# A row of table entries for the score banks of differential attention, and a bank of its own for five heads' sums of squares

## The chip, the cores and the metric

One Trainium2 chip, one core. The metric is the device time of one execution in microseconds (us), the median of several runs. TensorE is called PE here, VectorE DVE, ScalarE ACT, GpSimd POOL and SyncE SP, as in the profile. PSUM, the memory that PE writes and ACT and DVE read, has eight banks of 512 float32 per partition.

## The reference, cut to what matters

The kernel computes two transformer blocks of two layers each on 512 tokens of width 1024. The change touches one step of it, the differential attention of the second block: 8 heads, each with two score maps whose softmaxes are subtracted, and an RMS norm of each head's output over its 128 values.

```python
q_blk = q[:, i * BLOCK:n_k]
s = jnp.einsum('bqhcd,bkhcd->bhcqk', q_blk, k[:, :n_k]).astype(f32) * scale
s = jnp.where(kpos[None, :] <= qpos[:, None], s, -jnp.inf)
p = jax.nn.softmax(s, axis=-1)
a = p[:, :, 0] - lam * p[:, :, 1]
outs.append(jnp.einsum('bhqk,bkhe->bqhe', a.astype(v.dtype), v[:, :n_k]))
...
o = rms_norm_2(o, sub_gain) * (1.0 - lam_init)
```

The blocks i of 128 queries are causal: block b sees (b + 1) * 128 keys.

## The kernel before, in words

The whole kernel is one program in which every engine has its own instruction list, and semaphores hold them together. `X.wait_ge(e["name"], past(n))` lets engine X go on when n steps called "name" are done. An engine takes its instructions in their order, so a wait holds up all that stands behind it.

The differential attention is the functions `diff` of each engine: PE at line 1480, ACT at 2149, DVE at 2853, POOL at 859. Its unit is the **slot** s, one head h and one block b of queries: s = 4h + i, with b = i in head 0 and b = 3 - i in the others (`diff_slot`, line 728). So a head begins with its widest slot, of 512 keys, and ends with its narrowest, of 128. There are 32 slots. For one slot:

- PE `scores(s)` (lines 1510 to 1530) makes both maps c = 0, 1 with four matmuls each, of which one adds the mask. It waits until slot s - 3 has been read (`probs` past 2s - 4).
- DVE `neg_max(s)` (line 2889) takes the maxima of both maps from PSUM, and ACT `probs(s)` (line 2152) makes two exponentials of it, from PSUM to the tile tmp.
- DVE `combine(s)` (line 2897) forms the difference of the two maps. PE `turn_map(s)` (line 1532) transposes it in b + 1 blocks of 128 into bank 6, and ACT `take_map(s)` (line 2163) copies bank 6 to the tile Z.

Once a head: PE `values(h)` (line 1542) multiplies the four transposed maps with the values into bank 7. ACT `square(h)` (line 2171) squares bank 7. PE `mean_square(h)` (line 1551) sums these squares over the partitions with a matmul of ones (line 1556, two instructions) and adds the eps term in four small ones (line 1559, eight instructions), all into bank 6. ACT `scale(h)` (line 2177) makes a logarithm of bank 6 (line 2181) and an exponential (line 2184), which is the factor of the RMS norm. DVE `sub_norm(h)` and ACT `y_high(h)` use it.

Bank 6 therefore serves two things, the transposed maps and the sum of squares. Two waits keep them apart: `mean_square(h)` waits until the map before it has been taken (line 1554), and `turn_map` waits for the logarithm (line 1537).

The scores have banks 0 to 5, two banks a slot, in turn (`diff_pair`, line 736). From slot 20 on (line 733) a table gives them banks 0 to 4, where a slot of at most 256 keys has both maps in one bank. Bank 5 is then free for `fill`: from slot 24 on PE puts six matmuls of the output projection into every slot (lines 1487 to 1508, call at 1574), which write bank 5 (and bank 4 at the end).

The order of the work on PE is written out by hand at lines 1564 to 1578. In step s stand `turn_map(s - 3)`; then, in the last step of a head, `mean_square(h - 1)`; then `scores(s + 2)`; in the third step of a head `values(h - 1)`; and from step 24 on `fill(6)`. ACT's order is at lines 2196 to 2217: in step s `square(h - 1)` in the last step of a head, `scale(h - 2)` in the first, then `take_map(s - 3)`, then `probs(s)`.

Of the kernel before, what the change touches and what calls it, by code (L numbers as in the profile page):

```python
# [12 lines left out]
ACT = mybir.ActivationFunctionType  # L13
AX = mybir.AxisListType

P = 128
S = 512
# [3 lines left out]
NB = S // P  # L21
# [101 lines left out]
def program(nc, a, out):  # L123
# [9 lines left out]
    def past(n):  # L133

        return n + CR

    with ctx:
# [31 lines left out]
        ones = onesr[:, :].bitcast(F32)  # L169
        sq9 = sb("squares", [P, 5 * P])  # L170
        ident, ntri, nones, cos_rows, sin_rows = (sq9[:, k * P:(k + 1) * P] for k in range(5))
# [49 lines left out]
        PS = ctx.enter_context(nc.psum_tensor("banks", [P, 8 * S], F32))  # L221
        bank = [PS[:, j * S:(j + 1) * S] for j in range(8)]
        G = bank[0:2]

        def zt(k, n=1):
            return Z[:, k * S:(k + n) * S] if isinstance(k, int) else Z[:, bass.ds(k * S, n * S)]
# [419 lines left out]
        def tile_evac(st, b):  # L646

            return st.base // 2 + b // 2
# [76 lines left out]
        DIFF_SLOTS = 8 * NB  # L725
        BEHIND = 3
# [3 lines left out]
            h, i = divmod(s, NB)  # L730
            return h, i if h == 0 else NB - 1 - i

        PACKED = 5 * NB
        packed = dict(enumerate(((0, 1), (2, 3), (4,), (0,), (1, 2), (3, 4), (0,), (2,), (3, 4), (0, 1), (2,), (3,)), PACKED))

        def diff_pair(s):

            o = packed[s][0] if s >= PACKED else 2 * ((s + 1) % 3)
            step = S // 2 if s >= PACKED and len(packed[s]) == 1 else S
            return PS[:, o * S:o * S + 2 * step].rearrange("p (c n) -> p c n", n=step)  # L740

        def diff_scores(s, c):

# [2 lines left out]
        def fill_bank(l):  # L746

            return bank[4 if l in (5, 7) else 5]

        def fill_order(l):  # L750

            return {0: None, 6: 4, 7: 5}.get(l, l - 1 if l != 5 else None)
# [23 lines left out]
        def diff_eps(s, n=1):  # L776

            return sums8[:, 28 + s % 8:28 + s % 8 + n]
# [204 lines left out]
        def _(pe):  # L983
# [259 lines left out]
            for c in range(DC):  # L1243
# [3 lines left out]
                for b in range(NB):  # L1247
                    mm = pe.transpose(bank[5 + c % 2][:, b * P:(b + 1) * P], Z[:, 6 * S + b * D + c * P:6 * S + b * D + (c + 1) * P], ident)
# [231 lines left out]
            def diff(st):  # L1480
                e = df
                last = next(st for st in panels if st.ends == "diff")
                pe.wait_ge(h_take, past(last.tiles))

                filled = [0]

                def fill(n):

                    for m in range(filled[0], filled[0] + n):
                        l, i = divmod(m, 3 * FILL)  # L1490
                        k, part = divmod(i, 3)
                        par, u = l % 2, st.base + l
                        if i == 0:
                            if fill_order(l) is not None:
                                old = st.base + fill_order(l)
                                pe.wait_ge(evac[old % 2], past(old // 2 + 1))
                            if l == 5:
                                pe.wait_ge(e["probs"], past(2 * DIFF_SLOTS - 6))
                            if l == 0:
                                pe.wait_ge(e["output_high"], past(FILL))  # L1500
                                pe.wait_ge(e["output_low"], past(FILL))
                            pe.wait_ge(s_whi, past(u + 1))
                            pe.wait_ge(s_wlo, past(u + 1))
                        w, y = ((whi, yhi), (wlo, yhi), (whi, ylo))[part]
                        mm = pe.matmul(fill_bank(l), w[par][:, k * P:(k + 1) * P], ch(y, k), start=i == 0, stop=i == 3 * FILL - 1)
                        if i == 3 * FILL - 1:
                            mm.then_inc(gemm, 1)
                    filled[0] += n

                def scores(s):  # L1510

                    h, b = diff_slot(s)
                    n = (b + 1) * P
                    q_hi, q_lo, k_hi, k_lo = diff_parts(h)
                    pe.wait_ge(e["low_parts"], past(3 * h + 3))
                    if s in (NB, 2 * NB):
                        zero_rows_in(4)
                    if s in (1, 2):
                        for tile in (2 * s - 2, 2 * s - 1):
                            pe.wait_ge(evac[tile % 2], past(tile_evac(last, tile) + 1))  # L1520
                    pe.wait_ge(e["probs"], past(2 * s - 4))
                    qh, ql = q_hi[:, b * P:n], q_lo[:, b * P:n]
                    for c in range(2):
                        z = diff_scores(s, c)[:, 0:n]
                        kh, kl = k_hi[c][:, 0:n], k_lo[c][:, 0:n]
                        pe.matmul(z, qh, kh, start=True, stop=False)
                        pe.matmul(z, qh, kl, start=False, stop=False)
                        pe.matmul(z[:, b * P:n], identb[:, :], mask(M_C), start=False, stop=False, skip_group_check=True)
                        mm = pe.matmul(z, ql, kh, start=False, stop=True)
                    mm.then_inc(e["scores"], 1)  # L1530

                def turn_map(s):

                    h, b = diff_slot(s)
                    pe.wait_ge(e["combined"], past(s + 1))
                    pe.wait_ge(e["taken"], past(s))
                    pe.wait_ge(e["log_mean"], past((s + BEHIND - NB) // NB))
                    for kb in range(b + 1):
                        mm = pe.transpose(bank[6][:, kb * P:(kb + 1) * P], diff_probs(s, 0)[:, kb * P:(kb + 1) * P], ident)
                    mm.then_inc(e["turned"], 1)  # L1540

                def values(h):

                    pe.wait_ge(e["taken"], past(NB * h + NB))
                    pe.wait_ge(e["normed"], past(h))
                    for kb in range(NB):
                        mm = pe.matmul(bank[7][:, kb * P:S], zt(16 + h)[:, kb * P:(kb + 1) * P], zt(24 + kb)[:, kb * P:S],
                                       start=kb == 0, stop=kb == NB - 1, skip_group_check=True)
                    mm.then_inc(e["values_added"], 1)

                def mean_square(h):

                    pe.wait_ge(e["squares"], past(h + 1))
                    pe.wait_ge(e["taken"], past(min(NB * h + 2 * NB - BEHIND, DIFF_SLOTS)))
                    pe.wait_ge(e["eps_scaled"], past(h + 1))
                    pe.matmul(bank[6], ones, zt(28), start=True, stop=False, skip_group_check=True)
                    for s in range(NB * h, NB * h + NB):
                        _, b = diff_slot(s)
                        mm = pe.matmul(bank[6][:, b * P:(b + 1) * P], diff_eps(s).to_broadcast([P, P]), ident, start=False, stop=s == NB * h + NB - 1, skip_group_check=True)
                    mm.then_inc(e["mean_square"], 1)  # L1560

                scores(0)
                scores(1)
                for s in range(DIFF_SLOTS + BEHIND):
                    h, i = divmod(s, NB)
                    if s >= BEHIND:
                        turn_map(s - BEHIND)
                    if i == NB - 1 and h:
                        mean_square(h - 1)
                    if s + 2 < DIFF_SLOTS:  # L1570
                        scores(s + 2)
                    if i == (BEHIND - 1) % NB and h and s >= BEHIND:
                        values(h - 1)
                    if s >= 6 * NB:
                        fill(6)
                fill(12)
                mean_square(7)
                fill(18)

# [28 lines left out]
            for t in range(NB):  # L1608
                for hh in range(2):
                    n = 2 * t + hh  # L1610
                    if n >= 2:
                        pe.wait_ge(s_xc, DC + n - 1)
                    for c in range(4):
                        cc = 4 * hh + c
                        mm = pe.transpose(bank[n % 2][:, c * P:(c + 1) * P], xT[:, cc * S + t * P:cc * S + (t + 1) * P], ident)
# [5 lines left out]
        def _(act):  # L1621
# [527 lines left out]
            def diff(st):  # L2149
                e = df  # L2150
# [26 lines left out]
                def scale(h):  # L2177

                    act.wait_ge(e["mean_square"], past(h + 1))
                    act.wait_ge(e["rms_scale"], past(h))  # L2180
                    act.activation(zt(29), bank[6], ACT.Ln, scale=1.0 / P).then_inc(e["log_mean"], 1)
                    act.wait_ge(e["log_mean"], past(h + 1))
                    act.wait_ge(e["normed"], past(h))
                    act.activation(zt(30), zt(29), ACT.Exp, scale=-0.5).then_inc(e["rms_scale"], 1)
# [11 lines left out]
                for s in range(DIFF_SLOTS + BEHIND):  # L2196
                    h, i = divmod(s, NB)
# [814 lines left out]
```

## Time and profile before

| | us |
|---|---|
| three runs | 2924.63, 2926.41, 2929.20 |
| median | 2926.41 |
| span of the profiled execution | 2926.4 |
| differential attention in it | from 1418.9 to some 1543 |
| PE busy in the whole span | 2833.6 (97%) |

The profile gives the span of the profiled execution, from its first to its last instruction, and no other time of it. In a timeline a row has the start of an instruction, its duration, the engine and line, what it writes and reads, its shape and count; at the end, in brackets, stands the idle time of the engine before it and what released it. A PE row's duration runs over into the next one's start, since matmuls are pipelined: from start to start is what an instruction takes of PE's time.

### The profile page before, as it was taken

How to read it: one execution, taken by the hardware profiler on the slowest of the kernel's cores; microseconds unless marked ns; L12 is line 12 of the kernel's file. 1: busy time of each engine (PE TensorE's matmuls, PEld its weight loads, DVE VectorE, ACT ScalarE, POOL GpSimd, SP SyncE). 2: the span in 40 equal slices, each digit the busy share in tenths (PEclk: the TensorE clock that was granted, in tenths of full speed). 3: DMA queues.
4: the chain of work that ended last, by engine and by line, in shares of the span. 5: the costliest groups of instructions: out<-in, count | busy, mean ns of one | idle time of the engine just before them, and what ended most of it. 6: DMA issues, size and time to landing. Idle time of an engine off the chain costs nothing.

```text
span 2926.4 us, 39107 instructions
## 1 busy us (share of the span) xinstructions
PE 2833.6 (97%) x13399; PEld 2315.3 (79%) x13399; DVE 1744.8 (60%) x2111; ACT 1224.7 (42%) x2067; POOL 1079.0 (37%) x498
## 2 busy tenths in 40 slices
PE   6999999999899999999899999999999999999999
PEld 5767788887677888888667888888888888888887
DVE  7486777775566554668566333557566766644333
ACT  3574432224554322244454222356566665522221
POOL 1312344443213444444324444443412442244443
PEclk9999999999999999999999999999999999999999
DMA  6355263643112333332003333323301321133332
GB/s 218 88 167 193 79 203 98 208 127 105 37 30 79 93 99 95 94 95 87 29 26 97 94 94 95 99 88 91 92 23 53 95 87 30 51 94 94 101 94 93
DMA packets 366140, 278.96 MB, mean 95 GB/s; under 512 B 13618, under 2 KB 321203, under 8 KB 366003
## 3 DMA queue, kind: packets, MB, share of 16 engines
q1 hardware_dynamic: 364752, 276.83, 31.3%
q8 instruction: 82, 1.34, 0.2%
q14 instruction: 55, 0.45, 0.0%
q10 hardware_dynamic: 1251, 0.33, 0.0%
HBM read 275.03 MB, written 2.10 MB: 95 GB/s over the span
## 4 chain that ended last, share of the span: by engine, by line
PE 65%; issue 4%; DVE 2%; ACT 2%; POOL 1%; DMA 0%; POOLq 0%; DVEq 0%; ACTq 0%; SPq 0%
PE banks L1187 13%; PE banks L1182 12%; PE banks L1191 12%; PE banks L1050 6%; PE banks L1056 6%; PE banks L1053 6%; PE banks L1456 2%; PE banks L1023 1%; PE banks L1396 1%; PE banks L1184 1%; POOL w_lo L895 1%; PE banks L1385 0%; PE banks L1091 0%; PE banks L1431 0%; PE banks L1430 0%
## 5 line engine op out<-in xcount | busy, mean ns | idle before, releaser
L895 POOL TENSOR_TENSOR w_lo<-w_raw,w_hi 128x1024 fp32r<-128x1024 f32 (+2 forms) x431 | 1028.3, 2386 | 1693.2 <-ACT w_hi L1704 1692.2
L1704 ACT ACTIVATE w_hi<-w_raw 128x1024 fp32r<-128x1024 f32 (+2 forms) x432 | 447.3, 1035 | 1125.8 <-PE banks L1191 793.2
L1050 PE MATMUL banks<-w_hi,h_hi 128*128 128x512 f32 x960 | 386.4, 402 | 0.1
L1056 PE MATMUL banks<-w_lo,h_hi 128*128 128x512 f32 x960 | 376.7, 392 | 1.5 <-POOL w_lo L895 1.5
L1053 PE MATMUL banks<-w_hi,h_lo 128*128 128x512 f32 x960 | 375.2, 391 | 0.7 <-DVE h_lo L601 0.7
L1182 PE MATMUL banks<-h_hi,w_hi 128*128 128x512 f32 x1280 | 341.8, 395 | 7.1 <-ACT h_hi L1885 4.2
L1187 PE MATMUL banks<-h_lo,w_hi 128*128 128x512 f32 x1280 | 321.3, 391 | 2.4 <-DVE h_lo L601 2.3
L1182 PEld LDWEIGHTS banks<-h_hi,w_hi 128*128 128x128 f32 x1280 | 243.1, 190 | 65.0 <-issue 7.6
L1187 PEld LDWEIGHTS banks<-h_lo,w_hi 128*128 128x128 f32 x1280 | 240.5, 188 | 57.6 <-DVE h_lo L601 8.2
L1191 PE MATMUL banks<-h_hi,w_lo 128*128 128x512 f32 x1152 | 284.5, 389 | 0.0
L1191 PEld LDWEIGHTS banks<-h_hi,w_lo 128*128 128x128 f32 x1152 | 216.3, 188 | 44.9
L1182 PE MATMUL banks<-mid_hi,w_hi 128*128 128x512 f32 x864 | 220.3, 394 | 7.7 <-ACT mid_hi L1837 4.7
L1056 PEld LDWEIGHTS banks<-w_lo,h_hi 128*128 128x128 f32 x960 | 195.8, 204 | 36.9 <-POOL w_lo L895 3.2
L1053 PEld LDWEIGHTS banks<-w_hi,h_lo 128*128 128x128 f32 x960 | 196.6, 205 | 31.6 <-DVE h_lo L601 1.0
L1187 PE MATMUL banks<-mid_lo,w_hi 128*128 128x512 f32 x864 | 218.2, 391 | 2.3 <-DVE mid_lo L2394 2.1
L1050 PEld LDWEIGHTS banks<-w_hi,h_hi 128*128 128x128 f32 x960 | 196.1, 204 | 30.6 <-issue 0.5
L1191 PE MATMUL banks<-mid_hi,w_lo 128*128 128x512 f32 x864 | 214.4, 389 | 0.0
L2411 DVE TENSOR_TENSOR xT<-banks,xT 128x512 f32 (+1 forms) x80 | 55.3, 691 | 263.3 <-PE banks L1191 261.7
L1182 PEld LDWEIGHTS banks<-mid_hi,w_hi 128*128 128x128 f32 x864 | 160.7, 188 | 45.8 <-ACT mid_hi L1837 8.1
L1187 PEld LDWEIGHTS banks<-mid_lo,w_hi 128*128 128x128 f32 x864 | 162.2, 188 | 41.4 <-DVE mid_lo L2394 4.7
L1191 PEld LDWEIGHTS banks<-mid_hi,w_lo 128*128 128x128 f32 x864 | 162.2, 188 | 33.5
L2404 DVE TENSOR_TENSOR mid_lo<-tmp,mid_hi 128x512 f32 (+1 forms) x64 | 122.8, 1918 | 55.6 <-ACT mid_hi L1837 55.6
(373 smaller groups left out, 4272.8 us busy)
## 6 DMA issues: line engine op xcount, KB each, us to landing
Z<-in_ada_w SPq DMA_DIRECT2D x64, 512.0 KB, 5.2
w_raw<-in_m_w_up SPq DMA_DIRECT2D x64, 512.0 KB, 3.9
w_raw<-in_m_w_down SPq DMA_DIRECT2D x64, 512.0 KB, 3.6
w_raw<-in_kv_w SPq DMA_DIRECT2D x48, 512.0 KB, 3.8
w_raw<-in_ffn_w_gate SPq DMA_DIRECT2D x44, 512.0 KB, 3.7
w_raw<-in_ffn_w_up SPq DMA_DIRECT2D x44, 512.0 KB, 3.6
tmp<-in_ada_w SPq DMA_DIRECT2D x32, 512.0 KB, 4.4
w_raw<-in_ffn_w_down SPq DMA_DIRECT2D x32, 512.0 KB, 3.7
```

What stands on the lines that cost most here:

```text
L895: pool.tensor_tensor(wlo[j][:, 0:n], raw[j][:, 0:n], whi[j][:, 0:n], ALU.subtract).then_inc(s_wlo, 1)
L1023: mm = pe.transpose(turned(n)[:, j * P:(j + 1) * P], tmp[4 + n % 2][:, j * P:(j + 1) * P], ident)
L1050: pe.matmul(t, hh, wh, start=k == 0, stop=False)
L1053: pe.matmul(t, hl, wh, start=False, stop=False)
L1056: mm = pe.matmul(t, hh, wl, start=False, stop=k == DC - 1)
L1182: pe.matmul(g, whi[par][:, k * P:(k + 1) * P], hi[:, k * S:(k + 1) * S], start=(k == 0), stop=False)
L1187: mm = pe.matmul(g, whi[par][:, k * P:(k + 1) * P], lo[:, k * S:(k + 1) * S], start=False, stop=early and k == st.kc - 1)
L1191: mm = pe.matmul(g, wlo[par][:, k * P:(k + 1) * P], hi[:, k * S:(k + 1) * S], start=False, stop=(k == st.kc - 1))
L1456: mm = pe.matmul(o, dil_vals[:, at:at + P], dil_probs[q % 2][:, own:own + width], start=g == 0 and c == 0, stop=g == 2 and c == NB - 1, sk ...
L1704: act.activation(whi[par][:, 0:kc * P], raw[par][:, 0:kc * P], ACT.Copy).then_inc(s_whi, 1)
L2404: dve.tensor_tensor(ch(mlo, l), tmp[1], ch(mhi, l), ALU.subtract).then_inc(r_lo, 1)
L2411: dve.tensor_tensor(x, G[par], x, ALU.add).then_inc(evac[par], 1)
```

## The change

A table `PACKED` now gives the score banks of all 32 slots. Slots 0 and 1 have both maps in one bank each (2 and 3), slots 2 to 5 two banks each, slots 6 and 7 one bank each (5 and 4). Slots 8 to 31 use banks 0 to 4 alone, by the sequence that slots 20 to 31 had before. For heads 0 to 4 the sum of squares goes to bank 5 instead of bank 6. For these heads `mean_square` stands behind `scores(s + 2)` and not ahead of it, waits for the logarithm of the head before it and not for the map in bank 6, and `turn_map` waits for no logarithm. The first `fill`, which writes bank 5, waits for the logarithm of head 4. In slots 2 and 3 the waits for the banks of the stage before are changed to match the table. Heads 5 to 7 are as before.

```diff
-        PACKED = 5 * NB
-        packed = dict(enumerate(((0, 1), (2, 3), (4,), (0,), (1, 2), (3, 4), (0,), (2,), (3, 4), (0, 1), (2,), (3,)), PACKED))
+        PACKED = ((2,), (3,), (0, 1), (4, 5))
+        PACKED += ((2, 3), (0, 1), (5,), (4,))
+        ROUND = ((0, 1), (2, 3), (4,), (0,), (1, 2), (3, 4), (0,), (2,), (3, 4), (0, 1), (2,), (4,))
+        PACKED += ROUND + ROUND[:-1] + ((3,),)
+        OWN_MEANS = 5
 
         def diff_pair(s):
 
-            o = packed[s][0] if s >= PACKED else 2 * ((s + 1) % 3)
-            step = S // 2 if s >= PACKED and len(packed[s]) == 1 else S
-            return PS[:, o * S:o * S + 2 * step].rearrange("p (c n) -> p c n", n=step)
+            first, *second = PACKED[s]
+            step = (second[0] - first) * S if second else S // 2
+            return PS[:, first * S:first * S + 2 * step].rearrange("p (c n) -> p c n", n=step)
+
+        def diff_mean(h):
+
+            return bank[5 if h < OWN_MEANS else 6]
...
                             if l == 0:
+                                pe.wait_ge(e["log_mean"], past(OWN_MEANS))
                                 pe.wait_ge(e["output_high"], past(FILL))
...
-                    if s in (1, 2):
-                        for tile in (2 * s - 2, 2 * s - 1):
+                    if s in (2, 3):
+                        for tile in ((2, 3), (0, 1))[s - 2]:
                             pe.wait_ge(evac[tile % 2], past(tile_evac(last, tile) + 1))
...
                     pe.wait_ge(e["taken"], past(s))
-                    pe.wait_ge(e["log_mean"], past((s + BEHIND - NB) // NB))
+                    before = (s + BEHIND - NB) // NB
+                    if before > OWN_MEANS:
+                        pe.wait_ge(e["log_mean"], past(before))
...
                     pe.wait_ge(e["squares"], past(h + 1))
-                    pe.wait_ge(e["taken"], past(min(NB * h + 2 * NB - BEHIND, DIFF_SLOTS)))
+                    if h < OWN_MEANS:
+                        pe.wait_ge(e["log_mean"], past(h))
+                    else:
+                        pe.wait_ge(e["taken"], past(min(NB * h + 2 * NB - BEHIND, DIFF_SLOTS)))
                     pe.wait_ge(e["eps_scaled"], past(h + 1))
-                    pe.matmul(bank[6], ones, zt(28), start=True, stop=False, skip_group_check=True)
+                    pe.matmul(diff_mean(h), ones, zt(28), start=True, stop=False, skip_group_check=True)
...
                         turn_map(s - BEHIND)
-                    if i == NB - 1 and h:
+                    if i == NB - 1 and h > OWN_MEANS:
                         mean_square(h - 1)
                     if s + 2 < DIFF_SLOTS:
                         scores(s + 2)
+                    if i == NB - 1 and 0 < h <= OWN_MEANS:
+                        mean_square(h - 1)
...
-                    act.activation(zt(29), bank[6], ACT.Ln, scale=1.0 / P).then_inc(e["log_mean"], 1)
+                    act.activation(zt(29), diff_mean(h), ACT.Ln, scale=1.0 / P).then_inc(e["log_mean"], 1)
```

## Rows read from the trace of the kernel before

**Rows 1.** The page's first lines: span and PE's busy time.
```profile
span 2926.4 us, 39107 instructions
PE 2833.6 (97%) x13399; PEld 2315.3 (79%) x13399; DVE 1744.8 (60%) x2111; ACT 1224.7 (42%) x2067; POOL 1079.0 (37%) x498
```
**Rows 2.** The waits from 1442 to 1489 us: who waited for whom, total, times, longest.
```profile
PE banks L1526 <- ACT tmp L2160: 4.3, 8, 0.8
...
PE banks L1556 <- ACT Z L2175: 3.1, 4, 0.8
```
**Rows 3.** Busy time by stretch: start:end, length, engines, PE's granted clock, DMA.
```profile
1430.90:1436.30 5.40, 2.32 (x16) 1.62 (x15) 5.22 (x11) 3.64 (x10) 2.24 (x3) 1.00 0.00 0
1436.40:1439.80 3.40, 3.40 (x9) 2.17 (x10) 3.23 (x9) 1.06 (x5) 0.38 (x1) 0.50 0.00 0
1450.25:1462.66 12.41, 10.54 (x60) 7.51 (x61) 10.04 (x23) 7.98 (x26) 2.21 (x4) 1.00 0.00 0
1458.60:1462.66 4.06, 2.98 (x25) 2.51 (x24) 3.46 (x10) 3.69 (x13) 0.22 (x1) 1.00 0.00 0
```
**Rows 4.** Timeline of PE over one head, 1450.25 to 1462.66 us.
```profile
1450.25 0.47 PE L1526 MATMUL banks<-qk_parts 128*128 128x512 f32 x1 [0.26 <-ACT tmp L2160]
...
1452.02 2.39 PE L1547 MATMUL banks<-Z 128*128 128x512 f32 x8
1454.25 0.60 PE L1539 MATMUL banks<-squares,tmp 128*128 128x128 f32 x4
1455.64 1.10 PE L1556 MATMUL banks<-Z,ones_r 128*128 128x512 f32 x2 [0.78 <-ACT Z L2175]
...
1457.38 0.42 PE L1526 MATMUL banks<-qk_parts 128*128 128x384 f32 x1
...
1458.76 0.49 PE L1539 MATMUL banks<-squares,tmp 128*128 128x128 f32 x3
1459.01 0.36 PE L1526 MATMUL banks<-qk_parts 128*128 128x256 f32 x1
...
1460.05 0.38 PE L1539 MATMUL banks<-squares,tmp 128*128 128x128 f32 x2
1461.26 0.30 PE L1526 MATMUL banks<-qk_parts 128*128 128x128 f32 x1 [0.83 <-ACT tmp L2160]
...
1462.66 0.47 PE L1526 MATMUL banks<-qk_parts 128*128 128x512 f32 x1 [0.25 <-ACT tmp L2160]
```
**Rows 5.** Timeline of ACT in the same head.
```profile
1454.45 0.60 ACT L2175 ACTIVATE Z<-banks 128x512 f32<-128x512 f32 x1 [1.91 <-PE banks L1547]
1454.95 0.59 ACT L2168 ACTIVATE Z<-banks 128x512 f32<-128x512 f32 x1
...
1457.66 0.60 ACT L2181 ACTIVATE Z<-banks 128x512 f32<-128x512 f32 x1 [1.43 <-PE banks L1559]
1458.29 0.63 ACT L2184 ACTIVATE Z<-Z 128x512 f32<-128x512 f32 x1
1459.29 0.49 ACT L2168 ACTIVATE Z<-banks 128x384 f32<-128x384 f32 x1 [0.37 <-PE banks L1539]
1459.68 0.68 ACT L2160 ACTIVATE tmp<-banks,head_sums 128x512 f32<-128x512 f32 x1
...
1460.91 0.21 ACT L2160 ACTIVATION_READ_ACCUMULATOR tmp<-banks,head_sums 128x1 f32 x1
```
**Rows 6.** Timeline of PE where the fills begin, 1487.47 to 1498.79 us.
```profile
1487.47 0.47 PE L1526 MATMUL banks<-qk_parts 128*128 128x512 f32 x1 [0.25 <-ACT tmp L2160]
...
1496.23 0.36 PE L1526 MATMUL banks<-qk_parts 128*128 128x256 f32 x1
...
1497.27 0.39 PE L1505 MATMUL banks<-y_hi,w_hi 128*128 128x512 f32 x1
...
1498.79 0.31 PE L1526 MATMUL banks<-qk_parts 128*128 128x128 f32 x1
```

More of the change, by code:

```diff
@@ L1553, in mean_square @@
                     pe.wait_ge(e["squares"], past(h + 1))
-                    pe.wait_ge(e["taken"], past(min(NB * h + 2 * NB - BEHIND, DIFF_SLOTS)))
+                    if h < OWN_MEANS:
+                        pe.wait_ge(e["log_mean"], past(h))
+                    else:
+                        pe.wait_ge(e["taken"], past(min(NB * h + 2 * NB - BEHIND, DIFF_SLOTS)))
                     pe.wait_ge(e["eps_scaled"], past(h + 1))
-                    pe.matmul(bank[6], ones, zt(28), start=True, stop=False, skip_group_check=True)
+                    pe.matmul(diff_mean(h), ones, zt(28), start=True, stop=False, skip_group_check=True)
                     for s in range(NB * h, NB * h + NB):
                         _, b = diff_slot(s)
-                        mm = pe.matmul(bank[6][:, b * P:(b + 1) * P], diff_eps(s).to_broadcast([P, P]), ident, start=False, stop=s == NB * h + NB - 1, skip_group_check=True)
+                        mm = pe.matmul(diff_mean(h)[:, b * P:(b + 1) * P], diff_eps(s).to_broadcast([P, P]), ident, start=False, stop=s == NB * h + NB - 1, skip_group_check=True)
                     mm.then_inc(e["mean_square"], 1)
```

## The prediction

> **What bounds the kernel now.** I read the page first, then the waits of the stage, then one head on PE and ACT, because the kernel as a whole is PE's: it is busy for 97% of 2926.4 us [rows 1]. The change touches the differential attention alone, where PE is less full. One head of its steady part takes 12.41 us, of which PE is busy for 10.54, DVE for 10.04 and ACT for 7.98 [rows 3]. So 1.87 us a head are idle on PE, and the waits say where: 0.78 us ahead of the sum of squares, 0.83 ahead of the scores of the narrowest slot, 0.26 ahead of the widest slot's [rows 4]. Over four heads these are the 3.1 us for ACT's square and the 4.3 us for ACT's exponentials [rows 2].
>
> The reader should not stop at those 0.78 us. The question is which chain sets the 12.41 us. I follow it from the start of the widest slot's scores at 1450.25, called t = 0. PE goes on without a gap: those scores, then the values at t = 1.77, then the transposes of the widest map at t = 4.00 [rows 4]. ACT squares bank 7 at t = 4.20 and takes the widest map at t = 4.70, for 0.59 us, so until 5.29 [rows 5]. The sum of squares starts on PE at t = 5.39 [rows 4]. The timeline names the square (L2175) as its releaser, but that was over at 4.80; what came last was the taking of the map, the `taken` wait of line 1554. The sum takes until ACT's logarithm can start, t = 7.41, so 2.02 us; the exponential starts at 8.04 [rows 5]. PE meanwhile does the scores of 384 keys (t = 7.13) and three transposes (8.51) [rows 4], and ACT takes that map at t = 9.04, having waited 0.37 us for it [rows 5]. From there ACT does not stop: wide exponentials from 9.43 to 10.87 [rows 5], 0.14 us after which PE's narrow scores start (11.01), then the next map and the next exponentials, for which PE's next widest scores wait until t = 12.41 [rows 4]. So the head's period is 9.04 us up to ACT's taking of the three-block map, plus 3.37 us of ACT. Call the first part X. The 0.83 us on PE is the shadow of that ACT part, and is no time of its own.
>
> **The change, part by part.**
>
> *The table.* It moves slots 8 to 19 to five banks and packs the narrow slots. No instruction is added, and the wait for slot s - 3 is the old one; in the new table no bank comes back before that slot is read. What packing costs is in the trace, since slots 20 to 31 have it. The slot of 256 keys takes 1.04 us of PE unpacked (1459.01 to 1460.05) [rows 4] and 1.04 packed (1496.23 to 1497.27) [rows 6]. I take zero, for the narrower slot too. For slots 0 to 3, whose exponentials no row shows packed, I bound it by 0.1 us either way.
>
> *The waits of slots 2 and 3.* They are for banks that the previous stage has left; slot 2 waited for the same tiles before. Zero; covered by the 0.8 us or more of score matmuls ahead. Without that cover it would cost at most one copy of a tile, some 0.7 us (ACT's copies of 512 columns take 0.6 [rows 5]), once.
>
> *The sum of squares behind the scores.* In step 4h + 3 PE now does four transposes, scores of 384 keys, the sum. The transposes take some 0.35 us: three take 0.25 (1458.76 to 1459.01) and the fourth 0.1 more. Nothing holds the scores: the exponentials that they wait for ended before t = 2. So scores at t = 4.35, for 1.38 us (1457.38 to 1458.76) [rows 4], sum at 5.73. The square is done at 4.80, so PE waits for nothing: the 0.78 us of idleness is gone. But the sum starts at 5.73 and not at 5.39, which is 0.34 us later. The logarithm starts at 5.73 + 2.02 = 7.75 and the exponential 0.63 later, at 8.38.
>
> *Who waits behind it.* ACT's program has `scale` ahead of `take_map` and `probs`, so the late logarithm holds both. The three-block transpose no longer waits for the scores or the logarithm: PE has it done by 8.0. So X is now set by ACT itself: exponential at 8.38 plus the spacing to the next ACT instruction. That spacing is 0.50 by the pair square and taking, and 0.63 at most (the exponential's own length) [rows 5]. So X lies between 8.88 and 9.01, against 9.04. I take 8.91, by the first pair, which is the same form of instructions. The saving is 0.13 us a head, with ends 0.03 and 0.16. That is what is left of the 0.78 us. PE is then idle elsewhere: it finishes the scores of 256 keys at t = 8.76, waits some 0.6 us for ACT to take the map in bank 6, and 1.2 us for the wide exponentials (ending at 8.91 + 0.39 + 1.44 = 10.74), starting the narrow scores at 10.88 where it was 11.01.
>
> This holds for the sums of heads 0 to 3, four periods: 4 x 0.13 = 0.52 us.
>
> *The sum of head 4* comes before the first fill. There the time freed can be used. Before, from 1487.47 (t = 0), the narrow scores with a fill ahead of them start at 1498.79, t = 11.32, without idle time [rows 6]. After: sum ends at 5.73 + 1.74 = 7.47 (1455.64 to 1457.38), three transposes to 7.72, scores of 256 keys to 8.76, six fill matmuls and two transposes, 1.52 us (1497.27 to 1498.79), to 10.28, then the wait for the exponentials at 10.74 + 0.14 = 10.88. The gain is 11.32 - 10.88 = 0.44 us. Behind this point PE is bound by its own fills, so it is kept.
>
> *The wait added ahead of the first fill*, for the logarithm of head 4: done at 7.75 + 0.60 = 8.35, and the fill is reached at 8.76. Zero, by a cover of 0.4 us. If the cover were gone, the fill and the transposes and scores behind it would be late by as much, once. `mean_square`'s new wait for the previous logarithm is long satisfied. No DMA is moved, and SP and POOL have nothing that hangs on these waits.
>
> *The first eight slots* keep PE's order, so nothing goes there.
>
> **The sum:** 0.52 + 0.44 = 0.96 us, so 2926.4 - 1.0 = 2925.4 us against the profiled span [rows 1], which equals the median of the three runs. By the ends it is 0.1 + 0.3 = 0.4 us to 0.64 + 0.47 = 1.1 us. A measurement of this kernel can tell about 0.2%, 5.9 us, from no change.
>
> **Rivals.**
>
> *Nothing, or a little back* (2926.4 to 2926.9). If ACT's spacing behind an exponential is its full length and the sum takes longer in the stream than after a pause, X is 9.04 or above, and only head 4 gains. Each 0.1 us of X is 0.4 us in all. Against it: the spacing of 0.50. Chance 0.2.
>
> *All idle time of PE goes* (2917.0). Five heads at 1.87 us are 9.4 us. It would need ACT not to bind; but ACT waits only 0.37 us between its logarithm and the end of the chain [rows 5]. To pass 5.9 us it needs 1.2 us a head, nine times what I find. Chance 0.03. The Trainium skill's page Perfetto Trace Analysis, section Matmul Optimizations, asks that all eight PSUM banks be used to raise parallelism, and by it these 2917.0 us would be due; before and after, all eight are in use, and the rows put the limit on ACT's order.
>
> *PE's clock falls, slower* (2933.9). PE's granted clock was 0.50 from 1436.4 to 1439.8, its lower level of 1.2 GHz, after a stretch of 5.40 us in which PE was busy for only 2.32 [rows 3]. Today the thinnest stretch of a steady head has 2.98 busy in 4.06 [rows 3] and stays at 2.4 GHz. The change gathers the idle time: from t = 8.8 to 12.3 PE would be busy for some 1.7 of 3.5 us. A fall would hit the wide scores and the values, which are on the chain, and costs half of 3.4 us, 1.7. Five falls are 8.5 - 1.0 = 7.5 us slower; four (5.8) would still read as no change, so the rival decides only from five on. For it: that is about as thin as the stretch ahead of the fall. Against it: it must come in every head. Chance 0.04; one or two falls, 2927.1 or 2928.8, have 0.2. The same page's section also says that PE's clock follows its use, so that matmuls should run back to back, and TensorE: Matmul & The Clock Gate, in its section on depth-cycling, tells of a clock that goes up and down where PE pauses often between groups. By that rule 2927.1 to 2933.9 us would come out; the steady heads, with a clock of 1.00 and three pauses each, do not bear it out so far.
>
> **Chances and range.** The forecast has 0.53, the first rival 0.2, one or two falls 0.2, five falls 0.04, all idle time 0.03. Faster by over 0.2%: 0.04, with a little for a shifted state elsewhere. Slower: 0.05. Within: 0.91. The runs before spread from 1.8 below their median to 2.8 above. The range takes 2925.4 less 1.8 and 1.1 for the bounds, and at the top one or two falls, 2927.1 to 2928.8, plus that spread in part: 2922.0 to 2930.0.
>
> **What would show it.** Right: the period from wide scores to wide scores 12.25 to 12.35; no idle time before L1556, which starts 5.7 us after the wide scores; ACT's taking of three blocks following the exponential without a wait for PE; PE idle some 0.6 us before the two-block transpose and 1.2 before the narrow scores; the narrow scores of the first fill step 10.9 after the wide ones. Wrong: a period under 12.1 or at 12.41 and above, a wait before the first fill, packed slots of 256 keys longer than 1.04, or a granted clock of 0.50 anywhere between 1445 and 1500.

## The result, and the profile after

The changed kernel takes 2933.14 us (median of 20 runs, 2929.75 to 2935.39), the kernel before 2927.86 us (20 runs, 2924.44 to 2930.34). The ratio is 1.0018, with a 95% interval of 1.0012 to 1.0024: 5.3 us slower. The forecast was 2925.4 us and the range ended at 2930.0.

The page of the kernel after, its first lines:

```profile
span 2933.4 us, 39107 instructions
## 1 busy us (share of the span) xinstructions
PE 2844.7 (97%) x13399; PEld 2321.8 (79%) x13399; DVE 1745.7 (60%) x2111; ACT 1223.0 (42%) x2067; POOL 1075.9 (37%) x498
```

PE executes the same 13399 matmuls as before [rows 1], and yet is busy for 11 us more. The same matmuls have become longer. The busy time by stretch shows where (columns: start:end, length, busy PE, PEld, DVE, ACT, POOL, PE's granted clock, DMA share, GB/s). First the kernel after, ahead of the differential attention, in it and behind it:

```profile
0.00:1421.39 1421.39, 1366.23 (x6244) 1088.03 (x6245) 929.53 (x988) 570.59 (x972) 508.74 (x225) 0.99 0.37 114
1421.39:1549.92 128.53, 115.03 (x577) 82.45 (x576) 86.58 (x180) 69.31 (x201) 31.54 (x38) 0.92 0.06 17
1549.92:2933.40 1383.48, 1363.47 (x6581) 1151.34 (x6579) 729.58 (x944) 583.10 (x894) 535.62 (x235) 1.00 0.28 82
```

and the kernel before, in the same stage:

```profile
1418.95:1543.12 124.17, 108.19 (x578) 78.51 (x576) 86.57 (x180) 70.48 (x201) 33.12 (x38) 0.99 0.06 18
```

The stage is 4.36 us longer, at a granted clock of 0.92 instead of 0.99. Behind it nothing differs. Ahead of it, where both kernels do the same, this execution is 2.4 us longer: near 770 and 790 us, in a stage that the change doesn't touch, PE's clock is at its lower level for 17.1 us in two falls, where it is for 10.2 us in one in the kernel before. Inside the stage, stretches of the kernel after:

```profile
1442.40:1452.60 10.20, 8.49 (x53) 6.49 (x52) 7.04 (x16) 7.03 (x21) 0.47 (x1) 1.00 0.01 2
1452.65:1456.05 3.40, 3.40 (x9) 1.81 (x8) 2.91 (x7) 1.19 (x5) 1.31 (x3) 0.50 0.00 0
1456.05:1466.30 10.25, 8.54 (x53) 6.51 (x52) 7.43 (x18) 6.54 (x20) 0.50 (x1) 1.00 0.00 0
1466.30:1469.70 3.40, 3.40 (x9) 1.80 (x8) 2.89 (x7) 1.22 (x5) 1.33 (x3) 0.50 0.01 2
1480.00:1483.35 3.35, 3.35 (x9) 1.80 (x8) 2.82 (x7) 1.19 (x5) 1.31 (x3) 0.50 0.00 0
1493.65:1497.00 3.35, 3.35 (x9) 1.80 (x8) 3.28 (x6) 1.21 (x5) 2.99 (x5) 0.50 0.00 0
```

Once in each of heads 3 to 6, at its beginning, PE's clock falls to its lower level, 1.2 GHz, for 3.4 us. The timeline of PE over one of these heads, to be read beside [rows 4]:

```profile
1452.35 0.52 PE L1534 MATMUL banks<-qk_parts 128*128 128x512 f32 x1 [0.25 <-ACT tmp L2175]
...
1455.28 2.71 PE L1557 MATMUL banks<-Z 128*128 128x512 f32 x8
1457.82 0.60 PE L1549 MATMUL banks<-squares,tmp 128*128 128x128 f32 x4
1458.18 0.42 PE L1534 MATMUL banks<-qk_parts 128*128 128x384 f32 x1
...
1459.56 1.02 PE L1569 MATMUL banks<-Z,ones_r 128*128 128x512 f32 x2
...
1461.31 0.49 PE L1549 MATMUL banks<-squares,tmp 128*128 128x128 f32 x3
...
1463.29 0.41 PE L1549 MATMUL banks<-squares,tmp 128*128 128x128 f32 x2 [0.53 <-ACT Z L2183]
1464.63 0.30 PE L1534 MATMUL banks<-qk_parts 128*128 128x128 f32 x1 [0.93 <-ACT tmp L2175]
...
1466.03 0.53 PE L1534 MATMUL banks<-qk_parts 128*128 128x512 f32 x1 [0.25 <-ACT tmp L2175]
```

The pause ahead of the sum of squares (L1569) is gone, and a new one of 0.53 us stands ahead of the two-block transposes, with 0.93 and 0.25 behind it: as foretold, the idle time has moved to the end of the head (0.6 and 1.2 us were worked out). The wide scores now take 2.93 us (1452.35 to 1455.28) where they took 1.77, and the values 2.54 instead of 2.23. That is 1.47 us more than before, and the period is 13.68 us instead of 12.41. The stretch ahead of the fall, in the kernel after:

```profile
1462.75:1466.30 3.55, 1.84 (x13) 1.48 (x13) 2.40 (x6) 3.55 (x13) 0.50 (x1) 1.00 0.00 0
```

and the same part of a head in the kernel before:

```profile
1459.10:1462.66 3.56, 2.48 (x21) 2.02 (x20) 3.33 (x10) 3.37 (x12) 0.22 (x1) 1.00 0.00 0
```

PE is busy for 1.84 of 3.55 us where it was for 2.48 of 3.56.

The falls are not an affair of one profile. The granted clock over the whole span is 0.990 to 0.992 in the 20 runs of the kernel after (mean 0.9911) and 0.992 to 0.995 in the 83 runs of the kernel before that ran beside the experiments (mean 0.9935). Four stretches of 3.4 us at half the clock would lower this mean by 0.0023.

### The profile page after: what moved, and what is told of

It is laid out like the page before. It is cut to its first block, busy times and chain, and to the rows that moved or that the text cites. A ratio compares the mean times of both kernels' runs of the same rounds, so it can differ in the third digit from the quotient of the medians.

```text
span 2933.4 us, 39107 instructions
## 1 busy us (share of the span) xinstructions
PE 2844.7 (97%) x13399; PEld 2321.8 (79%) x13399; DVE 1745.7 (60%) x2111; ACT 1223.0 (42%) x2067; POOL 1075.9 (37%) x498
## 4 chain that ended last, share of the span: by engine, by line
PE 65%; issue 4%; DVE 2%; ACT 2%; POOL 1%; DMA 0%; POOLq 0%; DVEq 0%; ACTq 0%; SPq 0%
PE banks L1194 12%; PE banks L1189 12%; PE banks L1198 12%; PE banks L1057 6%; PE banks L1063 6%; PE banks L1060 6%; PE banks L1463 2%; PE banks L1030 1%; PE banks L1403 1%; PE banks L1191 1%; POOL w_lo L902 1%; PE banks L1392 1%; PE banks L1098 0%; PE banks L1438 0%; PE banks L1437 0%
```

## The experiments

Theory A: the change by itself would gain a little, and the four falls cost 4 x 1.47 = 5.9 us. Rivals: the table costs time (B), the shared bank's removal does (C), or the late logarithm on ACT does. Where the first expectation says heads 1 to 4, these are the four whose falls lie at the wide scores of heads 3 to 6. Each kernel below was run 6 to 12 times beside the kernel before on one chip; ratios are against the kernel before. The period is the time from one head's wide scores to the next one's on PE.

### The table alone

```diff
-        OWN_MEANS = 5
+        OWN_MEANS = 0
```

> The changed kernel's table of score banks, but every sum of squares in bank 6 and ahead of the scores, as before. Theory A (the loss of 5 us is PE's clock falling to its lower level once in each of heads 1 to 4, because the idle time of PE now lies together): no such falls, since the order is the old one; 0 us against the kernel before, period from wide scores to wide scores 12.4. Theory B (the five banks or the packed slots cost time): 4 to 5 us slower than before, with longer packed slots or new waits in front of scores.

Ratio 1.0007 (0.9998 to 1.0016). A head:

```profile
1451.26:1463.66 12.40, 10.53 (x60) 7.51 (x61) 10.03 (x23) 7.98 (x26) 2.21 (x4) 1.00 0.00 0
```

Period 12.40 and PE's busy time 10.53, as in [rows 3]. The table costs nothing in the steady heads; B falls by these rows, since the interval of the ratio ends at 1.0016 and would leave room for its 4 us. In head 2, which ends ahead of them, this profile has 14.24 us (1437.02 to 1451.26) where the kernel before has 13.90, with a fall of 6.8 us instead of 3.4; whether the table has a part in that isn't shown.

### The own bank, with the sum ahead of the scores

```diff
-                    if i == NB - 1 and h > OWN_MEANS:
+                    if i == NB - 1 and h:
                         mean_square(h - 1)
...
-                    if i == NB - 1 and 0 < h <= OWN_MEANS:
-                        mean_square(h - 1)
```

> The changed kernel, but with the sum of squares ahead of scores(s + 2), as before; its own bank and the two waits less stay. The sum then waits for the square alone and starts 4.9 us after the wide scores instead of 5.4. Worked out as in the prediction, the three-block map is taken at 8.55 and the period is 11.9. Theory A: the idle time of PE is 1.7 us a head, 0.3 of it ahead of the sum, so less lies together and the clock holds: 2 to 3 us faster than before. If it falls all the same: 12.4 + 0.9 = 13.3 a head, 3 to 5 us slower. Theory C (it is the shared bank's removal and not the place of the sum that costs): as slow as the changed kernel, 5 us slower than before, with the clock at its upper level.

Ratio 0.9993 (0.9984 to 1.0002). Timeline of PE over a head, and its busy time:

```profile
1467.02 1.13 PE L1569 MATMUL banks<-Z,ones_r 128*128 128x512 f32 x2 [0.25 <-ACT Z L2188]
...
1472.69 0.30 PE L1534 MATMUL banks<-qk_parts 128*128 128x128 f32 x1 [0.83 <-ACT tmp L2173]
1474.08 0.47 PE L1534 MATMUL banks<-qk_parts 128*128 128x512 f32 x1 [0.25 <-ACT tmp L2173]
```

```profile
1462.17:1474.08 11.91, 10.58 (x60) 7.51 (x61) 10.03 (x23) 7.97 (x26) 2.21 (x4) 1.00 0.01 3
```

The sum starts 4.85 us after the wide scores (1467.02 - 1462.17), waiting for the square alone; before it waited for the taken map as well, as the prediction read. The period is 11.91 where 11.9 was worked out. The own bank is worth 0.5 us a head, and C falls; the whole kernel's ratio stands for 2 us, as expected, but its interval reaches 1.0002 and doesn't confirm them.

### The changed kernel, its pauses filled

```diff
+                def feed(h, n):
+
+                    pe.wait_ge(e["log_mean"], past(h))
+                    for _ in range(n):
+                        pe.matmul(bank[5], identb[:, :], maskb[:, 0:S], start=True, stop=True)
...
+                    feeding = i == 1 and 2 <= h <= 5
+                    if feeding:
+                        feed(h - 1, 2)
                     if s >= BEHIND:
                         turn_map(s - BEHIND)
+                    if feeding:
+                        feed(h - 1, 4)
```

> The changed kernel with matmuls of no use (128 x 512, bf16, into bank 5) in PE's two pauses of each of heads 2 to 5's second step: two ahead of the transposes and four ahead of the narrow scores. Nothing else is changed. Theory A: PE's granted clock holds at 1.00 from 1445 to 1500, the period is 12.2 to 12.3 and the kernel is 5.5 to 7 us faster than the changed one, so 0.5 to 1.5 us faster than before. If the clock has nothing to do with it: added work can only keep the time or lengthen it, 5 us or more slower than before.

Ratio 0.9993 (0.9984 to 1.0002), against 1.0018 (1.0012 to 1.0024) without these matmuls. A head:

```profile
1463.33:1475.40 12.07, 11.60 (x65) 7.99 (x67) 10.18 (x23) 7.75 (x26) 1.83 (x4) 1.00 0.01 3
```

Six matmuls more a head, and the head is 1.6 us shorter (12.07 against 13.68); that is what one fall costs, since the transposes of the widest map start 3.87 us after the wide scores here and 5.47 there. The clock stays at 1.00. This is the decisive run: the work of the change, its waits and its order on every engine are untouched, but for one wait of the added matmuls, for the logarithm that reads bank 5. It was over when they were reached (1471.48 us, the first of them at 1472.20). The 12.07 is also the price of the change without falls, 0.34 us a head less than before.

### The second pause alone filled

Against the kernel just shown:

```diff
-                        feed(h - 1, 2)
+                        feed(h - 1, 0)
```

> The changed kernel with only the second of the two pauses filled: four matmuls of no use ahead of the narrow scores, none ahead of the two-block transposes. Theory A: what counts is how much idle time lies together, and some 0.9 us of the 1.8 are gone, less than the kernel before has: the clock holds, period 12.1 to 12.2, 1 to 2 us faster than before. If any pause ahead of the transposes were the trigger: falls as in the changed kernel, 5 us slower than before.

Ratio 0.9992 (0.9983 to 1.0001). Two heads:

```profile
1459.85:1484.00 24.15, 22.33 (x126) 15.73 (x129) 20.36 (x45) 15.51 (x50) 3.67 (x7) 1.00 0.01 1
```

The 0.5 us pause ahead of the transposes is left, with the added wait in it, and the clock holds. So it is the four matmuls ahead of the narrow scores that hold it, and neither that pause nor that wait.

### The order alone

```diff
-        OWN_MEANS = 5
+        OWN_MEANS = 0
...
-                    if i == NB - 1 and h > OWN_MEANS:
+                    if i == NB - 1 and h > 5:
...
-                    if i == NB - 1 and 0 < h <= OWN_MEANS:
+                    if i == NB - 1 and 0 < h <= 5:
```

> The table with the sum of squares still in bank 6 (with the old waits), but behind scores(s + 2): the order alone. PE has to wait for the logarithm ahead of the three-block transposes, some 0.9 us at t = 7.5, and then for the exponentials at t = 9.8 to 11. Theory A: the pauses are spread as before, no falls in every head; period 12.3 to 12.5, within 1 us of before. If late logarithms alone cost (the order on ACT): 0.4 us or more a head, 2 us slower, and then the changed kernel's loss is in part its order.

Ratio 0.9995 (0.9986 to 1.0004). Timeline of PE, then the head, its last part and its thinnest part:

```profile
1470.31 0.52 PE L1549 MATMUL banks<-squares,tmp 128*128 128x128 f32 x3 [0.78 <-ACT Z L2196]
...
1472.84 0.30 PE L1534 MATMUL banks<-qk_parts 128*128 128x128 f32 x1 [0.83 <-ACT tmp L2175]
1474.24 0.47 PE L1534 MATMUL banks<-qk_parts 128*128 128x512 f32 x1 [0.26 <-ACT tmp L2175]
```

```profile
1462.01:1474.24 12.23, 10.36 (x61) 7.53 (x61) 10.18 (x23) 7.87 (x26) 1.84 (x4) 1.00 0.01 3
1470.70:1474.24 3.54, 2.45 (x22) 1.99 (x20) 2.13 (x5) 3.50 (x13) 0.23 (x1) 1.00 0.02 5
1469.50:1473.05 3.55, 1.94 (x16) 1.64 (x15) 1.75 (x6) 3.41 (x9) 0.00 (x0) 1.00 0.00 0
```

The place behind the scores costs nothing: the period is 12.23, less than 12.41. With the sum in bank 6, PE waits 0.78 us for the logarithm ahead of the three-block transposes, and its last 3.5 us stay 2.45 busy. The own bank takes this wait away, and a pause of 0.53 us comes about 1 us later, next to the one ahead of the narrow scores. So neither half of the change makes the clock fall; the two together do. But the amount of idle time in one stretch doesn't tell the two kernels apart: about 1 us earlier in the head, this one has a stretch with 1.94 of 3.55 us busy, nearly as thin as the 1.84 of the kernel after. It comes in each of these heads, and the clock stays at 1.00 through all of them. What in the pauses' amount and place decides isn't shown.

### Two heads instead of five

```diff
-        OWN_MEANS = 5
+        OWN_MEANS = 2
```

> The changed kernel with the own bank, and with it the place behind the scores, for heads 0 and 1 only instead of 0 to 4. Theory A (each such head gathers PE's idle time and brings one fall of the clock): two falls between 1445 and 1475 instead of four between 1445 and 1500, heads of 13.7 us for those two and 12.4 for the next two; the stage from the widest slot of head 3 to the end is 2.4 us longer than before, against 4.7 in the changed kernel. If the falls come from something that happens once (the start of the stage, a phase), they come in all heads or in none.

Ratio 1.0009 (1.0001 to 1.0018), half of 1.0018. Three heads in a row:

```profile
1448.34:1462.00 13.66, 11.94 (x61) 8.42 (x61) 10.36 (x23) 7.76 (x26) 1.84 (x4) 0.88 0.00 0
1462.00:1475.87 13.87, 12.00 (x61) 8.42 (x61) 9.33 (x22) 7.86 (x26) 1.83 (x4) 0.88 0.01 2
1475.87:1488.28 12.41, 10.54 (x61) 7.51 (x61) 10.03 (x23) 7.97 (x26) 2.21 (x4) 1.00 0.00 0
```

Two sums in the own bank, two falls, and then 12.41. From head 3's wide scores to head 7's it is 53.58 us, 2.7 more than in the kernel before (expected: 2.4), against 4.7 more in the kernel after. The mean granted clock of the 11 runs, 0.9921, lies between the 0.9911 of the kernel after and the 0.9935 of the kernel before.

### The logarithm late

ACT's `scale` of heads 0 to 3 stands behind `probs` in step 4h + 1, and DVE's `sub_norm` one step later.

```diff
-                    if i == 0 and h >= 2:
+                    if i == 0 and h >= 6:
                         scale(h - 2)
...
                         probs(s)
+                    if i == 1 and 2 <= h <= 5:
+                        scale(h - 2)
...
+                    if i == 2 and 2 <= h <= 5:
+                        sub_norm(h - 2)
                     if s:
                         combine(s - 1)
...
-                    if i == 1 and h >= 2:
+                    if i == 1 and h >= 6:
                         sub_norm(h - 2)
```

> The changed kernel, with ACT's logarithm and exponential of heads 0 to 3 moved behind the exponentials of the next slot but one (last in step 4h + 1), and DVE's use of them one step later. PE's order is the changed kernel's. Theory of the chain (ACT's order sets the period, the sum only through the logarithm that ACT puts ahead of its map and exponentials): the three-block map is then taken at 8.0 us as soon as it is transposed, and the period is 8.0 + 3.35 = 11.35 us instead of 12.1 to 12.2 without falls; PE's idle time shrinks to 1.4 a head and the clock holds; 4 to 5 us faster than before. If DVE or PE bound the head: the period stays at 12.0 or above. If the clock still falls: 12.8 a head.

Ratio 0.9988 (0.9979 to 0.9996). ACT's timeline, then the head:

```profile
1468.79 0.49 ACT L2183 ACTIVATE Z<-banks 128x384 f32<-128x384 f32 x1 [2.04 <-PE banks L1549]
...
1471.87 0.63 ACT L2196 ACTIVATE Z<-banks 128x512 f32<-128x512 f32 x1
```

```profile
1460.59:1472.16 11.57, 10.42 (x61) 7.48 (x61) 9.84 (x23) 7.73 (x25) 1.84 (x4) 1.00 0.01 3
```

ACT takes the three-block map at 8.20 (1468.79 - 1460.59; expected 8.0) and waits for PE there, not for its own logarithm. The period falls by 0.5 us against 12.07, to 11.57 (expected: 11.35), and the kernel is 3.5 us faster than before (expected: 4 to 5; the interval is 1 to 6). The clock holds in the steady heads. The chain of the prediction is confirmed: with PE's order unchanged, moving two ACT instructions, and the DVE one that uses them, gives more than the 0.34 us that the change did on PE.

### Logarithm and sum late

In addition to the edit just shown:

```diff
-                    if i == NB - 1 and h > OWN_MEANS:
+                    if i == NB - 1 and h >= OWN_MEANS:
                         mean_square(h - 1)
...
-                    if i == NB - 1 and 0 < h <= OWN_MEANS:
-                        mean_square(h - 1)
+                    if i == 0 and 2 <= h <= OWN_MEANS:
+                        mean_square(h - 2)
```

> As the one with the late logarithm, and PE's sum of squares of heads 0 to 3 is late too, behind scores(s + 2) of the next step (head 4's stands ahead of the scores, as before). PE then turns the three-block map at 5.7 us and ACT goes from one map and its exponentials to the next. By ACT's chain alone the period is 10.8; DVE's 10.04 busy and PE's some 9.9 are near: 10.8 to 11.3, 4.5 to 7 us faster than before, no falls. If the sum's place on PE no longer matters once the logarithm is late: as the other, 11.3.

Ratio 0.9980 (0.9972 to 0.9989), 5.9 us faster than before. The head, and DVE's use of the factor:

```profile
1460.43:1471.59 11.16, 10.31 (x61) 7.49 (x61) 9.81 (x23) 7.85 (x25) 2.20 (x4) 1.00 0.01 3
```

```profile
1461.48 0.75 DVE L2938 SCALAR_TENSOR_TENSOR y_tile<-banks,small,Z 128x512 f32<-128x512 f32 x1 [0.98 <-ACT Z L2199]
```

The period lies inside the expected 10.8 to 11.3. Now DVE waits 0.98 us for the exponential, and its end, 1462.23, is what PE's values (start 1462.37) follow.

### The first pauses filled

Every profile up to here has another fall, which begins between 1431 and 1437 us and lasts 3.4 or 6.8 us, behind the thin stretch of [rows 3]. Bank 7 is unused there.

```diff
+                    feed({5: 5, 6: 6}.get(s, 0))
                     if s >= BEHIND:
                         turn_map(s - BEHIND)
+                    feed({6: 2}.get(s, 0))
```

Here `feed(n)` puts n matmuls as above into bank 7. In the kernel with both parts late:

> The kernel with logarithm and sum late, and in PE's three pauses ahead of the first wide slot of head 2 (steps 5 and 6) 13 matmuls of no use into bank 7, which nothing uses yet. Theory A: the fall of the clock near 1431 to 1437, 3.4 or 6.8 us at 1.2 GHz in every profile so far, goes; the part from head 1's wide slot to head 3's shrinks by 1.4 to 3 us; 7 to 9 us faster than the kernel before. If the clock falls there for another reason: no change against the same kernel without them, about 6 us faster.

Ratio 0.9968 (0.9955 to 0.9980): 2919.25 us, median of 6 runs, beside 2927.85 for the kernel before on that chip. In the kernel before:

> The kernel before, with these 13 matmuls alone. Theory A: no fall near 1436, 1.4 to 3 us faster than before, steady heads still 12.4. Otherwise the time of before, or up to 1 us more.

Ratio 0.9994 (0.9984 to 1.0003). Head 2 in the kernel before, then in this one, then in the one with both parts late:

```profile
1436.35:1450.25 13.90, 12.02 (x60) 8.49 (x61) 9.61 (x24) 8.01 (x26) 0.65 (x2) 0.88 0.00 1
```

```profile
1435.81:1448.12 12.31, 10.44 (x61) 7.54 (x61) 9.61 (x24) 8.00 (x26) 0.66 (x2) 1.00 0.00 1
```

```profile
1434.45:1445.33 10.88, 10.09 (x61) 7.50 (x61) 10.40 (x25) 6.78 (x23) 1.18 (x2) 1.00 0.01 2
```

The fall is gone in both, worth 1.6 us in that head (13.90 to 12.31). In the kernel before the whole's ratio can't tell this from no change. The version with everything is the fastest found, and beats both kernels; against the one without the first feed its gain is 2.1 us in this head (13.00 to 10.88), and the two ratios' intervals overlap a little.

## Why the prediction was wrong

**The bound of a head.** Right. ACT's chain sets the period, through the logarithm ahead of its map; the late logarithm showed it, and so did the own bank, whose 11.9 us came from the same steps.

**Table, packing, the waits of slots 2 and 3.** Right for the table and the packed slots in the steady heads: zero (12.40). For the first slots, and so for the two waits, no run separates a cost of 0.3 us from the fall there.

**The sum behind the scores.** Right in direction, too small in size. Without falls the period is 12.07 and not 12.28, so the saving is 0.34 us a head and not 0.13. Two terms were off. The sum in the stream took 1.95 us to the logarithm and not 2.02, the value after a pause. And the values ended earlier: before, they started 0.14 us behind DVE's `sub_norm`, which reads the bank that they write, and which the prediction did not look at:

```profile
1463.55 0.74 DVE L2921 SCALAR_TENSOR_TENSOR y_tile<-banks,small,Z 128x512 f32<-128x512 f32 x1
```

It ended at 1464.29 and the values began at 1464.43. In the filled run it ends 1.36 us before them, at 1463.69, since DVE is earlier. The values then start 1.72 us after the wide scores and not 1.77, and take 2.15 us and not 2.23, together 3.87 and not 4.00; the same 2.15 stands in the kernel with the order alone. A third term was right by its size and not by its reason: 8.91 has 0.53 us between ACT's exponential and its taking of the map, while the pair that the prediction names for it is 0.50 apart (1454.45 to 1454.95), which gives 8.88. The filled run has 0.53.

**Where PE would be idle.** Right in place: 0.53 us (0.6 foretold) ahead of the two-block transposes, and 0.93 (1.2 foretold) ahead of the narrow scores.

**The first fill.** The new wait costs nothing, as foretold. Without falls the gain there, in the filled run, is 13.64 - 12.99 = 0.65 us, where 0.44 was worked out.

**The clock.** This is the step that failed: the sum has no term for falls of PE's clock, and from head 3 on the stage lost 4.7 us by them, net of the change's gain. The prediction named the mechanism, its place (wide scores and values) and its price (1.7 us, measured 1.6), saw that the stretch would be as thin as the one ahead of the fall near 1436, and then took the falls for chances that would have to come "in every head" one by one. It gave one or two falls 0.2 and five 0.04, and nothing at all to three or four, which is what happened. It also set the rival aside because the steady heads before kept their clock with three pauses each, though the change was about to move those pauses. The heads are copies of one another, and here the fall came in each of the four. (The fifth sum has the first fills behind it, and no fall.) In the profile after the falls stand 13.65 us apart, once in each of the four heads, always within 0.3 us of the start of the wide scores. The thin stretch, 1.84 busy in 3.55, was worked out as 1.7 in 3.5; the comparison with 2.48 in 3.56 of the same place before was not made. It would have been a warning and no proof, as the order alone shows with 1.94. Three heads of 13.67 us in place of 12.41 and the first fill's of 14.57 in place of 13.64 give 3.8 + 0.9 = 4.7 us, which is the stage's loss but for 0.3 us gained ahead of them.

**The base.** The span of an execution is some 1.7 us less than its time (the run of the profile after: span 2933.4, time 2935.14). The prediction took the profile's span, 2926.4, as the base, and called it equal to the median of three runs; the two quantities met by chance. The base of 20 runs is 2927.86, so 1.5 us of the 7.7 us of the miss come from there.

## What to carry to other kernels

Follow the chain before pricing a pause: taking PE's pause ahead of an operation away gives little while another engine's order sets the period, and the idle time turns up further on. Then ask where it turns up, because a new place of the pauses can cost PE's clock, and in a loop it can do so in every pass. A few matmuls of no use in such a pause are a cheap test of this, and moving the instruction that the real chain waits for (here a logarithm that nobody needs soon) is the better cure by the length of a head, 11.57 us against 12.07; the ratios of the whole kernel overlap.

## What was not expected of the hardware

PE's clock followed how its work was spread, at the same work in a head. In the kernel after PE was busy for 1.84 or 1.85 us of the 3.55 ahead of each of the four falls, and the clock was then at 1.2 GHz for 3.4 us; four matmuls in one pause of 0.9 us kept it at 2.4 GHz. Adding 24 matmuls made the kernel some 7 us faster (ratios 0.9993 and 1.0018 of 2928).

The busy time ahead of a fall does not foretell it. The clock held with 1.94 of 3.55 us busy, in the kernel with the order alone, and it fell behind a busier stretch of another stage, here in the kernel before:

```profile
914.05:917.60 3.55, 2.87 (x8) 1.10 (x6) 3.55 (x6) 0.66 (x1) 0.00 (x0) 1.00 0.00 0
917.60:921.00 3.40, 3.33 (x8) 2.51 (x8) 2.11 (x3) 1.06 (x1) 1.03 (x1) 0.50 0.00 0
```

So no share of busy time should be carried from here to another kernel; look at the granted clock of the stretch itself. Nor do the runs settle why the falls lie so near the start of the wide scores in all four heads, and so never miss one. A head with a fall is 13.67 us long, the distance between two falls is 13.65, and no run separates the one from the other.
